# A hybrid attention kernel: the correction matmul of the scores over 64 rows in place of 128

## The reference

```
h = rms_norm(x, norm_g)
proj = h @ w_in                      # cut into the heads' q, k, v and gates of three groups
A: 12 heads of 64, three dilated causal windows with the same q, k, v, mixed by their softmax sums
B:  8 heads of 64, causal softmax attention with a bias c[t] - c[s]
C:  4 heads, gated linear attention (GLA) in chunks, with an RMS norm of the output
mixed = concat(out_a * silu(az), out_b * silu(bz), out_c * silu(cz))
return x + mixed @ w_out
```

## Time and profile before

| | |
|---|---|
| time, median of 3 runs | 2314.66 us (2314.51 to 2315.89) |
| the profiled execution | 2314.51 us, of which the span is 2312.7 us |
| PE busy | 2190.4 us, 95% of the span, 11056 matmuls |
| PEld busy | 1841.8 us, 80% |
| DVE, ACT, POOL busy | 972.4, 859.2, 232.6 us |
| projection L1466 to L1468 | 5568 matmuls, 745.1 + 730.2 + 730.7 us |
| granted TensorE clock, mean | 0.972 of full speed |

### The profile page before, as it was taken

One profiled execution on the slowest core, in us unless ns is written; L12 is line 12 of the kernel. 1 busy time (PEld: TensorE's weight loads), 2 busy tenths in 40 slices (PEclk: granted clock), 3 DMA queues, 4 the chain that ended last, 5 costly groups with the idle time before them and its releaser, 6 DMA issues.

```text
span 2312.7 us, 30429 instructions
## 1 busy us (share of the span) xinstructions
PE 2190.4 (95%) x11056; PEld 1841.8 (80%) x11056; DVE 972.4 (42%) x1628; ACT 859.2 (37%) x1457; POOL 232.6 (10%) x139
## 2 busy tenths in 40 slices
PE   3999989898998999999999999999999978899999
PEld 3788878787787888888888888888888866778887
DVE  5511143443434454544445454545444456422122
ACT  5211124232425444444444444444444444321110
POOL 0100031304131000000101010000000010000000
PEclk8999989898989999999999999999999989999999
DMA  5122213131323122222212222222222234332233
GB/s 176 44 76 68 86 48 97 46 92 56 95 63 99 61 64 78 73 80 70 78 59 73 67 82 69 89 77 63 89 79 91 77 131 164 118 134 87 86 119 141
DMA packets 185433, 199.26 MB, mean 86 GB/s; under 512 B 15672, under 2 KB 134456, under 8 KB 184208
## 3 DMA queue, kind: packets, MB, share of 16 engines
q1 hardware_dynamic: 168640, 167.84, 23.8%
q10 hardware_dynamic: 16720, 30.45, 3.5%
HBM read 148.86 MB, written 49.38 MB: 86 GB/s over the span
## 4 chain that ended last, share of the span: by engine, by line
PE 78%; issue 6%; DVE 5%; DMA 4%; ACT 4%; POOL 2%; SPq 1%; ACTq 0%; DVEq 0%; POOLq 0%
PE acc L1466 16%; PE acc L1468 16%; PE acc L1467 15%; PE turned L1648 3%; PE pv L1661 3%; PE pv L1660 3%; PE scores L1637 2%; PE scores L1634 2%; DMA w_raw<-in_w_out_dram 1%; POOL q_level L673 1%; PE acc L1740 1%; PE acc L1742 1%; PE acc L1741 1%; PE pv L1542 1%; PE turned L1742 1%
## 5 line engine op out<-in xcount | busy, mean ns | idle before, releaser
L1466 PE MATMUL acc<-act_hi,w_hi 128*128 128x512 f32 x1856 | 745.1, 401 | 0.0
L1468 PE MATMUL acc<-act_hi,w_lo 128*128 128x512 f32 x1856 | 730.7, 394 | 0.0
L1467 PE MATMUL acc<-act_lo,w_hi 128*128 128x512 f32 x1856 | 730.2, 393 | 0.0
L1069 DVE TENSOR_TENSOR w_lo<-w_raw,w_hi 128x512 fp32r<-128x512 f32 x233 | 186.5, 800 | 634.6 <-ACT w_hi L724 633.8
L1468 PEld LDWEIGHTS acc<-act_hi,w_lo 128*128 128x128 f32 x1856 | 352.8, 190 | 77.8
L1467 PEld LDWEIGHTS acc<-act_lo,w_hi 128*128 128x128 f32 x1856 | 354.1, 191 | 68.5
L1466 PEld LDWEIGHTS acc<-act_hi,w_hi 128*128 128x128 f32 x1856 | 354.1, 191 | 68.3 <-DVE w_lo L1069 0.9
L724 ACT ACTIVATE w_hi<-w_raw 128x512 fp32r<-128x512 f32 x233 | 146.3, 628 | 382.1 <-PE acc L1468 307.2
L953 ACT ACTIVATE prob<-prob,neg_max 128x128 f32<-128x128 f32 (+7 forms) x160 | 124.4, 777 | 292.8 <-DVE neg_max L1299 292.8
L1315 DVE TENSOR_TENSOR pt_lo<-turned,pt_hi 128x128 fp32r<-128x128 f32 (+7 forms) x160 | 120.8, 755 | 157.6 <-ACT pt_hi L961 156.9
L1661 PE MATMUL pv<-pt_lo,v_st 128*128 128x128 f32 x720 | 170.2, 275 | 0.0
(11 more groups left out here) (246 smaller groups left out, 2804.6 us busy)
## 6 DMA issues: line engine op xcount, KB each, us to landing
w_raw<-in_w_in_dram SPq DMA_DIRECT2D x232, 256.0 KB, 2.8
proj_scratch<-stage ACTq DMA_DIRECT2D x116, 256.0 KB, 2.1
w_raw<-in_w_out_dram SPq DMA_DIRECT2D x94, 256.0 KB, 3.0
raw<-proj_scratch SPq DMA_DIRECT2D x20, 512.0 KB, 3.3
x_tile<-in_x_dram SPq DMA_DIRECT2D x8, 1024.0 KB, 4.8
raw<-mixed_scratch SPq DMA_DIRECT2D x16, 512.0 KB, 4.4
res<-in_x_dram SPq DMA_DIRECT2D x24, 256.0 KB, 5.8
out_dram<-res SPq DMA_DIRECT2D x24, 256.0 KB, 3.0
```

Of the source, the lines that this page charges most:

```text
L1069: dve.tensor_tensor(w_lo[:, slot, :], w_raw[:, slot, :], w_hi[:, slot, :].bitcast(F32), ALU.subtract)\
L1466: pe.matmul(bank[th][:], hi, xh, start=first, stop=False)
L1467: pe.matmul(bank[th][:], hi, xl, start=False, stop=False)
L1468: mm = pe.matmul(bank[th][:], lo, xh, start=False, stop=end)
```

## The change

The second matmul of each piece contracts only over the head's own 64 partitions: both its stationary operand (`q_st[own, h]`) and its moving operand (`k_lo[own]`) are 64 x 128 and 64 x n slices, on partitions 0 to 63 for h = 0 and 64 to 127 for h = 1. The zeros in `k_lo` aren't needed any more, so the two clears on GpSimd and the semaphore `k_zeroed` go, and `k_lo` is one buffer of 1024 columns with head 0 in its upper and head 1 in its lower half of partitions. `sq` gets an address of its own, and `sq_lo` is one buffer of 512 columns. The scratch of the pairs becomes 2 KB smaller in each partition. 

```diff
-        squares = ExitStack()
-        sq = sb("sq", [P, 2, HALF], scope=squares)
-        squares.close()
-        sq_lo = sb("sq_lo", [P, 2, HALF], F32R, scope=pairs)
+        sq = sb("sq", [P, 2, HALF], scope=pairs)
         sq_hi = sb("sq_hi", [P, HALF], F32R, scope=pairs)
+        sq_lo = sb("sq_lo", [P, HALF], F32R, scope=pairs)
...
-        k_lo = sb("k_lo", [P, 2, SEQ], F32R, scope=pairs)
+        k_lo = sb("k_lo", [P, SEQ], F32R, scope=pairs)
...
-                pool.tensor_tensor(k_lo[own, h, :], raw[own, 1, :], k_hi[own, h, :].bitcast(F32),
+                pool.tensor_tensor(k_lo[own, :], raw[own, 1, :], k_hi[own, h, :].bitcast(F32),
                                    ALU.subtract).then_inc(kl_done, 1)
 
-            pool.wait_ge(gla_out, 2 * C_HEADS)
-            for h in range(2):
-                pool.memset(k_lo[(1 - h) * HEAD:(2 - h) * HEAD, h, :].bitcast(F32), 0.0).then_inc(k_zeroed, 1)
...
-                dve.tensor_tensor(sq_lo[:, m % 2, :], sq[:, m % 2, :], sq_hi[:].bitcast(F32),
+                dve.tensor_tensor(sq_lo[:], sq[:, m % 2, :], sq_hi[:].bitcast(F32),
                                   ALU.subtract).then_inc(sq_lo_done, 1)
...
-                pe.matmul(side[:], half_ones_r[:], sq_lo[:, m % 2, :], start=False, stop=True).then_inc(ssq_done, 1)
+                pe.matmul(side[:], half_ones_r[:], sq_lo[:], start=False, stop=True).then_inc(ssq_done, 1)
...
-                if first_pair(pair) and i == 0:
-                    pe.wait_ge(k_zeroed, h + 1)
                 pe.wait_ge(masked, ITEMS * pair + j)
-                q = q_st[:, h, i * P:(i + 1) * P]
+                q, own = q_st[:, h, i * P:(i + 1) * P], slice(h * HEAD, (h + 1) * HEAD)
                 for c0 in range(0, n, HALF):
                     c1 = min(c0 + HALF, n)
                     pe.matmul(scores[:, c0:c1], q, k_hi[:, h, c0:c1], start=True, stop=False)
                     if kind == 1 and c1 == n:
                         pe.matmul(scores[:, i * P:n], ident_r[:], causal_r[:], start=False, stop=False)
-                    mm = pe.matmul(scores[:, c0:c1], q, k_lo[:, h, c0:c1], start=False, stop=True)
+                    mm = pe.matmul(scores[:, c0:c1], q_st[own, h, i * P:(i + 1) * P], k_lo[own, c0:c1], start=False,
+                                   stop=True)
                 mm.then_inc(s_done, 1)
```

More of the change, by code:

```diff
@@ L276, in build @@
             sem(n) for n in "dist_chain ws_hi_done ws_lo_done small_done small_out small_saved lf_step c_done".split())
-        c_saved, k_zeroed = sem("c_saved"), sem("k_zeroed")
+        c_saved = sem("c_saved")
         hi_done, lo_done, quarter_done, half_done, evac_done = (
```

## The result

The changed kernel takes 2391.44 us (median of 4 runs, 2390.25 to 2393.28) where the kernel before takes 2314.68 us (4 runs, 2314.51 to 2315.89): a ratio of 1.033, 95% interval 1.0316 to 1.0344, 76.8 us slower. The forecast was 2396, the range 2348 to 2420.

A forecast was written before the change was run, and what follows sets the result against it. TensorE was taken as the bound beside nine of ten pairs. 480 changes of shape add 85.5 us, 81 after the last pair hides half of its 8.5; 2314.5 + 81 gives about 2396 us, range 2348 to 2420.

The forecast's parts named there:

- The bound: Beside nine of ten pairs TensorE hardly stands still, so added time between matmul starts is kernel time; 77 us there.
- Nothing saved by fewer rows: Second score matmuls: streamed columns stay the same and loads hardly get shorter, so zero saved for matmul and load.
- The price of a change: Between 128-row and 64-row matmuls the load can't run ahead: +0.19 us behind 512, 384 or 256 columns, +0.145 behind 128.
- The way back: From a 64-row matmul to the next full one: 40 changes behind 128 columns, 200 behind more, same price assumed.
- the way in: From a full matmul to the 64-row second score matmul: 240 changes, load 0.31 us late behind 512 columns, +0.19 us.
- the rival of half the price: Rival for the score matmuls: only one side of each piece shows the gap, half the price; chance 0.15.
- The count: 240 second score matmuls make 480 changes: 128 at 0.145 us and 352 at 0.19 us, 85.5 us.
- The last pair: A tenth of the cost, 8.5 us, falls beside 24 us of idle time; half of it was to disappear.
- None: Rival: the gap at L1525 has another cause, or 64 rows behave as 128; about 2314.5 us, chance 0.06.
- Faster: Rival: loading half the rows takes half the time, 4.4 us saved at 128 and 256 keys; 2310 us, chance 0.02.
- Dearer: Rival: a change waits for the full latency, 2444 us, or gaps let the clock fall; chance 0.09.
- The clears on GpSimd: Two clears, 1.95 us at 713.41, are hidden by 35 us of other work; dropping them saves nothing.

The follow-up runs named there:

- the two doubled runs: Changed kernel with each 64-row matmul issued twice, 2429.48 us; control, the kernel before with its 128-row second score matmul issued twice, 2352.76 us.
- the first experiment: Kernel before with only the second score matmul cut to its own 64 partitions; zeros, clears, semaphore and buffers kept: 2391.79 us, ratio 1.0327.
- the grouped order: Changed kernel with the 128-row matmuls of both pieces of an item first, then the 64-row matmuls of both: 2363.30 us, ratio 1.0206.

## Why the prediction was right

**The bound.** That TensorE's starts set the time beside nine pairs held: from the first second-score matmul to the first of the last pair it is 1125.1 us before (750.69 to 1875.78) and 1201.5 us after (750.96 to 1952.44), 76.4 us more, where 77 were forecast. These are the matmuls between which the nine pairs and, further below, the last pair are measured (before, then after):

```profile
750.69 0.27 PE L1637 MATMUL scores<-k_lo,q_st 128*128 128x128 f32 x1
1875.78 0.41 PE L1637 MATMUL scores<-k_lo,q_st 128*128 128x128 f32 x1
2040.74 0.47 PE L1740 MATMUL acc<-w_hi,act_hi 128*128 128x512 f32 x1 [1.82 <-DVE sq L1407]
...
750.96 0.32 PE L1630 MATMUL scores<-k_lo,q_st 64*128 64x128 f32 x1
1952.44 0.47 PE L1630 MATMUL scores<-k_lo,q_st 64*128 64x128 f32 x1
2119.84 0.47 PE L1734 MATMUL acc<-w_hi,act_hi 128*128 128x512 f32 x1 [2.75 <-DVE sq L1402]
```

It is a stretch with no new wait for another engine: TensorE waits there only for VectorE's `v_st` and `sq_lo`, 11.5 us before and 8.0 us after. The closeness of 76.4 to 77 is in part luck, as the sum left these waits as they were: outside of them the stretch grew by some 80 us, 3 more than the sum has, and the shorter waits took about as much off.

**Nothing saved by fewer rows.** Right within the noise, by the two doubled runs.

**The price of a change.** The four prices were estimates, put together from the 0.31 us at L1525 and from spacings of other matmuls. The changed kernel shows each of them. These are the distances from the start of a second score matmul to the start of the matmul behind it, beside the nine pairs (medians in us, least and most in brackets, then how many):

| columns | forecast | changed kernel, 64 rows | kernel before, 128 rows | added |
|---|---|---|---|---|
| 512 | 0.42 | 0.428 (0.420 to 0.432), 108 | 0.229 | 0.199 |
| 384 | 0.365 | 0.365 (0.365 to 0.372), 36 | 0.179 | 0.186 |
| 256 | 0.31 | 0.310 (0.309 to 0.312), 36 | 0.118 | 0.192 |
| 128 | 0.255 | 0.253 (0.251 to 0.255), 36 | 0.113 | 0.140 |

The two parts show as well. The 64-row load behind a 512-column matmul of 128 rows whose own load ran ahead starts 0.318 us after that matmul (18 cases), where 0.31 was read at L1525; behind 384 columns it is 0.262 us (12 cases), behind 128 it is 0.150 (median of 54). And the load itself, 0.11 us from its start to the next one in the earlier trace rows, is now waited for, as at L1461 above. The prediction calls 0.19 us the price measured on a change of rows. Measured there was the 0.31 us alone: L1525 is listed 0.32 us behind L1468, within 0.01 us of its own load, and the 0.11 us were added as an estimate.

**The way back.** This was the weak step, since the only row for it, at L1531, was blurred by a wait for ScalarE. It was assumed to cost as much as the way in, and it does: 775.45 to 775.88 is a way back behind 512 columns, and 776.14 to 776.39 one behind 128. With it the rival of half the price fell: by the same prices the ways in alone would add 41.6 us (88 x 0.145 + 152 x 0.19) and the ways back alone 43.8 (40 x 0.145 + 200 x 0.19), about 2357 us. The lower end of the range, 2348, lies below that; the runs showed both ways, and 2391.44 us.

**The count.** 480 changes, of which 160 go when the two pieces are grouped: 28 to 30 us measured for 30 by the sum. Head 0 alone gives 41 us for half of the changes, 42.7 by the sum before anything disappears in the last pair.

**The last pair.** Here the sum was off, if little. Of the 8.5 us that its 48 changes cost, half were to disappear in its waits. From its first second-score matmul to the first matmul of the last stage (L1740, L1734 after) the kernel before takes 2040.74 - 1875.78 = 165.0 us and the changed one 2119.84 - 1952.44 = 167.4 us: 2.4 us more, so nearly three quarters seem to have been covered; no run separates the last pair. The forecast 2396 is 4.6 us too high in all. About 2 us come from here, about 0.5 each from the nine pairs and from rounding 2395.5 up, and 1.8 from the profiled execution: 2393.28 us is the longest of the four, 1.8 above their median. So in the medians the slowdown is 76.8 us, and 79.1 us in the profiled spans.

**The rivals.** "None": the gap at L1525 might have come from its four waits or another cause. It fell: with the rows alone changed, and no wait, the loads stop and the time grows by 75.5 us. "Faster", by a shorter load: a load of 64 rows takes 0.18 us where one of 128 takes 0.19, and two of them are 0.11 us apart in both. "Dearer", by the full latency or the clock: a change behind 512 columns adds 0.199 us, not 0.27, and the clock is 1.00 beside the nine pairs before and after. The clears on GpSimd: in the first experiment they are still there, and the time is the same as without them.

**Still open.** Of the 0.428 us from load to load behind 512 columns, 0.23 is the columns' own distance and 0.11 that of two loads; that leaves about 0.09 us. No run varies these apart, and none shows what TensorE does in the 0.09 us. Whether a change from the part at row 0 to the part at row 64 costs the same wasn't run, nor were 64-row matmuls of the two heads side by side on the two halves of the array. No version with 64 rows beats the kernel before: the grouped order is the best of them, and still 2% slower.

## What to carry to other kernels

A contraction over half of the partitions saved no time here, on a bound TensorE, where it stands between full ones: the columns cost the same, and each change of the row part cost 0.14 us (behind 128 columns) to 0.2 us (behind 512). Padding the idle half with zeros, as the kernel before does, was the cheap form, 2314.68 us against 2391.44; if the padding can't be had, group the matmuls of the same shape (28 us less here), and look for such changes in the load row of the timeline, since the page's busy time hides them. Count changes, not matmuls.

## What the runs showed of the hardware

The asymmetry of rows and columns was open before the runs: 480 changes between 128 and 64 array columns cost nothing (0.9981, 0.9971 to 0.9990), 480 between 128 and 64 rows cost 75.5 to 76.8 us. And 96 rows behave as 128 (1.0006). That the price is so regular was unexpected as well: the 0.31 us of one row at L1525, on a float32 matmul of 16 rows, with 0.11 us added for the load, gave the price for float32r matmuls of 64 rows to a hundredth of a microsecond. For the way back that price was an assumption that happened to hold. The two types differ in pace: matmuls of 512 columns with both operands in float32r (`F32R` in the kernel, L1466) are followed by the next one after 0.227 us (median), the float32 ones at L1525 after 0.429 us.
